# A 31-tap causal convolution split between TensorE and VectorE: 16 and 15 taps in place of 19 and 12

## What is computed

```
proj = h @ w_in[l]
a_val, a_gate, u_pool, gate_a, gate_b = jnp.split(proj, ...)
ya = a_val * jax.nn.sigmoid(a_gate)              # 256 x 512
ya = causal_dwconv(ya, w_dw_a[l], b_dw_a[l])     # 31 taps, each channel by itself
ya = jax.nn.silu(layer_norm(ya, ln_a_g[l], ln_a_b[l]))
ya = ya @ w_pw_a[l]
pooled = causal_multiscale_pool(u_pool)
yb = jnp.einsum("bsgc,gcd->bsgd", pooled, w_pool[l]).reshape(...) * pool_scale[l]
merged = jax.nn.sigmoid(gate_a) * ya + jax.nn.sigmoid(gate_b) * yb
mix = merged @ w_out[l]
```

## Time and profile before

| | us |
|---|---|
| median of 3 runs | 1150.93 |
| the runs | 1148.71, 1150.93, 1152.8 |
| the profiled execution, its time | 1148.73 |
| its span, from the first to the last instruction | 1146.9 |
| PE busy / DVE busy / ACT busy in the span | 1090.2 / 792.9 / 601.2 |

### The profile page before, as it was taken

One profiled execution on the slowest core, in us unless ns is written; L12 is line 12 of the kernel. 1 busy time (PEld: TensorE's weight loads), 2 busy tenths in 40 slices (PEclk: granted clock), 3 DMA queues, 4 the chain that ended last, 5 costly groups with the idle time before them and its releaser, 6 DMA issues.

```text
span 1146.9 us, 19072 instructions
## 1 busy us (share of the span) xinstructions
PE 1090.2 (95%) x7816; PEld 1021.5 (89%) x7816; DVE 792.9 (69%) x1363; ACT 601.2 (52%) x1016; POOL 3.3 (0%) x13
## 2 busy tenths in 40 slices
PE   7998989999999999879989999999999899999997
PEld 7998878899999989779988799999899787999996
DVE  7988488878877788686675755555688747455555
ACT  5567435465565547643354644454565546444453
POOL 0000000000000000000000000000000000000000
PEclk9999999999999998989999999999999999999999
DMA  9985246346666624233222456555555335555520
GB/s 371 418 330 176 92 148 257 107 153 244 245 210 218 199 79 140 69 104 131 74 92 88 149 172 190 193 184 198 170 184 166 111 110 186 191 189 182 190 73 37
DMA packets 58550, 195.56 MB, mean 171 GB/s; under 512 B 10848, under 2 KB 11232, under 8 KB 58208
## 3 DMA queue, kind: packets, MB, share of 16 engines
q1 hardware_dynamic: 58464, 194.35, 49.6%
HBM read 193.01 MB, written 1.31 MB: 169 GB/s over the span
## 4 chain that ended last, share of the span: by engine, by line
PE 74%; DVE 17%; ACT 6%; issue 2%; SPq 1%; DMA 0%; POOL 0%; ACTq 0%; DVEq 0%; POOLq 0%
PE ps L542 61%; DVE lo L1644 5%; PE ps L816 4%; ACT hi L1119 2%; DVE raw L1631 2%; PE ps L644 2%; PE ps L699 1%; DVE ev L1875 1%; PE ps L537 1%; DVE ev L1872 1%; PE ps L549 1%; DVE B L1653 1%; PE ps L822 1%; DVE B L2039 1%; DVE B L1759 1%
## 5 line engine op out<-in xcount | busy, mean ns | idle before, releaser
L1644 DVE TENSOR_TENSOR lo<-raw,hi 128x1024 fp32r<-128x1024 f32 x311 | 377.1, 1221 | 171.5 <-ACT hi L1119 170.5
L542 PE MATMUL ps<-hh,hi 128*128 128x256 f32 x1568 | 447.8, 286 | 14.6 <-DVE hl L1736 3.2
L542 PE MATMUL ps<-hh,lo 128*128 128x256 f32 x1568 | 441.3, 281 | 0.0
L542 PE MATMUL ps<-hl,hi 128*128 128x256 f32 x1568 | 441.1, 281 | 0.0
L1119 ACT ACTIVATE hi<-raw 128x1024 fp32r<-128x1024 f32 x311 | 322.9, 1051 | 55.2 <-PE ps L542 55.1
L542 PEld LDWEIGHTS ps<-hh,hi 128*128 128x128 f32 x1568 | 298.4, 190 | 20.0 <-issue 10.0
L542 PEld LDWEIGHTS ps<-hl,hi 128*128 128x128 f32 x1568 | 298.3, 190 | 1.9
L542 PEld LDWEIGHTS ps<-hh,lo 128*128 128x128 f32 x1568 | 298.3, 190 | 0.0
L1350 ACT ACTIVATE ev<-ps 128x256 f32<-128x256 f32 x72 | 27.7, 385 | 109.9 <-PE ps L542 109.9
L542 PE MATMUL ps<-hi,fh 128*128 128x512 f32 x192 | 76.3, 398 | 0.0
L542 PE MATMUL ps<-lo,fh 128*128 128x512 f32 x192 | 75.9, 395 | 0.0
(11 more groups left out here) (274 smaller groups left out, 1332.6 us busy)
## 6 DMA issues: line engine op xcount, KB each, us to landing
raw<-in_w SPq DMA_DIRECT2D x359, 512.0 KB, 4.3
B<-in_t SPq DMA_DIRECT2D x2, 512.0 KB, 4.9
xa<-in_x SPq DMA_DIRECT2D x1, 1024.0 KB, 10.5
B<-in_r SPq DMA_DIRECT2D x1, 1024.0 KB, 7.1
out<-h SPq DMA_DIRECT2D x4, 256.0 KB, 2.0
cst<-in_c SPq DMA_DIRECT2D x1, 928.0 KB, 8.5
B<-between SPq DMA_DIRECT2D x32, 4.0 KB, 1.7
vec<-in_v SPq DMA_DIRECT2D x1, 328.5 KB, 6.6
```

The costliest lines, as they stand in the source:

```text
L542: m = g.matmul(o, l, r, start=first and n == 0, stop=last and n == 2, skip_group_check=True)
L1644: g.tensor_tensor(lo[:, j % SPLIT, :], raw[:, PLACE[j] % RAW, :], hi[:, j % SPLIT, :].bitcast(F), ALU.subtract).then_inc(*up("lo", j))
```

## The change

Taps 12, 13 and 14 move from TensorE to VectorE. TensorE's groups 9, 10 and 11 have one tap in place of two. VectorE does two taps in each of its turns 4, 5 and 6 in place of one: taps 9 and 10, 11 and 12, 13 and 14. The joining addition waits for VectorE's tap 14 in place of 11.

```diff
-        PE_TAPS = list(range(12, 31))
-        TAPS_AT = {n: t for n, t in zip(range(1, 13), (1, 1, 1, 2, 2, 1, 2, 2, 2, 2, 2, 1))}
+        PE_TAPS = list(range(15, 31))
+        TAPS_AT = {n: t for n, t in zip(range(1, 13), (1, 1, 1, 2, 2, 1, 2, 2, 1, 1, 1, 1))}
...
                 if n < 7:
-                    tap(4 + n if n < 2 else 5 + n)
+                    for i in (4 + n,) if n < 2 else (5 + n,) if n < 4 else (2 * n + 1, 2 * n + 2):
+                        tap(i)
...
                 s.wait_ge(*at("conv", (30, 3)))
-                s.wait_ge(*at("tap", (11, 3)))
+                s.wait_ge(*at("tap", (14, 3)))
```

## The result

The changed kernel takes 1149.0 us (median of 20 runs) and the kernel before 1151.3 us (20 runs). The ratio is 0.9974 with a 95% interval of 0.9962 to 0.9986: 3.0 us less (1.6 to 4.4), where 5.2 were forecast. Weighted by their half widths (1.4, 1.8 and 1.6 us) the three make 3.4 us, give or take 0.9, so 5.2 lies outside; each of the two later comparisons alone would just admit it (up to 5.3 and 5.5). The change is faster, but a good third of its gain is missing.

A forecast was written before the change was run, and what follows sets the result against it. TensorE was taken to bound the long convolution's stretch; three taps at 1.73 us take 5.19 us off the path, VectorE's added work hidden in waits. 1150.3 less 5.19 gives 1145.1 us, range 1141.5 to 1149.

The forecast's parts named there:

- TensorE's term: In the long convolution, three taps leave TensorE in groups 9, 10 and 11: 3 x 1.73 = 5.19 us off the path.
- VectorE's turns: Two taps in turns 4, 5 and 6, 4.74 us added, fit into VectorE's waits; it ends 0.88 us before TensorE.
- The other end: VectorE's operations at 477 ns each, a pair of taps 3.82 us, VectorE 0.26 us behind TensorE: gain 4.93 us.
- The step that failed: Behind the convolution only the start moves; the next projection's first matmul stays 14.14 us after the addition, span 5.19 us shorter.
- the rival for "slower": Clock halved from the next projection's first matmul for its 96 passes: 11.5 us more, 1156.6 us; chance 0.03.
- The other rival about the clock: After the convolution, one more low-clock stretch eats up to 3.4 us of the gain: around 1148.5 us; chance 0.11.
- The level: Base for the whole kernel: mean of four executions, 1150.3 us, from which 5.19 was taken to give 1145.1.

The follow-up runs named there:

- the two later comparisons: The changed kernel, run unchanged twice more against the kernel before: ratios 0.997 and 0.9966, so 3.5 and 3.9 us less.
- the ladder: One, two, three or four taps moved from TensorE to VectorE, against the kernel before: ratios 0.9994, 0.9972, 0.9974 (first comparison) and 0.9933.
- the shift: 15 matmuls on the idle tile ahead of TensorE's last tap, in the kernel before (1154.18 us) and in the changed kernel (1147.42 us).
- the filling: 60 in place of 38 matmuls on the idle tile ahead of the next projection: kernel before 1152.33 us, changed kernel 1145.67, four taps moved 1143.69.

## Why the prediction was wrong

- **TensorE's term** was right. Three times 1.73 us left the path, in the three groups named, and the joining addition came 5.19 us earlier when the 0.2 us between the executions are taken off.
- **VectorE's turns** were right turn by turn: waits of 1.53 us in turn 5 (1.5 forecast) and none in turn 6, a pair of taps at 3.17 us (3.16), slack 0.89 (0.88). The other end weighed there, each operation at its full recorded 477 ns, would have made a pair 3.82; two taps in direct succession don't cost that. The prediction took that end for the rule of the Trainium skill (VectorE: DVE Perf Modes, "The DRAIN you can't avoid"), but gave only half of it: the section says that the next operation waits for an empty pipe, and also that one that is not held starts earlier. The trace of the changed kernel, with 0.396 us from start to start, agrees with the second part.
- **The step that failed** is the one behind the convolution: "TensorE idles there now too and loses nothing". The idle time is indeed the same 2.8 us, but whether it costs clock depends on when it comes, and the change moved it to where it does. It cost 1.54 us in each of three traces. The kernel before lost nothing at this place in two traces, but did lose it (10.20 us for the 72 matmuls) once 15 matmuls had moved the place by 1.75 us; the changed kernel with the same 15 matmuls took 8.66 again.
- **The rivals.** The fall of the clock at exactly this place stood there as the rival for "slower", with 3 in 100. The place was right; the price of 11.5 us supposed that the low clock would last through the projection, where it lasted 3.4 us. The other rival about the clock, a part of the gain eaten, with 11 in 100, is nearest to what happened. It named no place, priced a stretch at up to 3.4 us where this one cost 1.54, and took the stretches for chance. I argued against it that as many stretches can vanish as appear. For a single idle stretch that is moved by a fixed amount, that was wrong. What I leaned on was the Trainium skill (TensorE: Matmul & The Clock Gate, "Part 1"), which says that the gate doesn't start anew with the kernel and that the number of slow matmuls varies from run to run. The traces here agree that executions of one kernel differ (a mean clock of 0.983, 0.983 and 0.981 in the three of the changed one). That the losses therefore even out at a given place was my own step, and the traces disagree with it: the outcome here was the same in three traces of one kernel and in two of the other.
- **The sum with this term:** 5.19 - 1.54 = 3.65 us, or 3.5 with the 0.17 us around the span, against 3.4 measured over three comparisons. Within the first comparison, 3.0 (1.6 to 4.4), it fits too.
- **The level.** The forecast of 1145.1 started from a mean of four executions, 1150.3. Over 20 runs the kernel before has 1151.3, so another 1.0 us of the miss is the base. The profiled execution of 1148.73 us is very likely the first of the three runs, 1148.71, counted twice; the mean of the three is 1150.8.

What stays open: each trace is one execution, so that the half-clock stretch falls here in the timed runs as well is inferred from the times of the ladder and the shift, not seen in each. Moving the idle time moves everything behind it as well, and the filling, which was to test this one gap alone, came with another half-clock stretch ahead of it; so the share of this gap in the timed gain rests on the traces and on the sum coming out. The half-clock stretches further behind also differ between traces (the first pair ended only 1.1 us apart in span, the second pair 2.8). From the last of the projection's 72 matmuls to the end of the span the kernel before takes 985.8 and 988.3 us, the changed kernel 988.6, 988.5 and 989.0, and the other variants between 987.0 and 990.8. What the change does to that part, if anything, no run tells. Why a gap is caught at one place and not at another isn't shown either.

## What to carry to other kernels

Shortening work on the path moves every idle stretch of TensorE behind it, and such a stretch (here 2.8 us, ahead of dense matmuls) can start or stop costing clock by being moved. So look at the granted clock right behind each such gap before and after, price a caught one from a row (here 1.54 us for 3.4 us at half clock), and judge an edit by several sizes of it: one, two, three and four taps gave -0.7, -3.2, -3.4 and -7.7 us. VectorE's work that stayed inside its measured waits was free, and carrying the order of time forward by hand foretold what was left of them to some hundredths of a microsecond.

## What was not expected of the hardware

The half-clock stretch at the projection recurs in place relative to the work in all three traces of the changed kernel, within some 0.3 us of the first matmul, although one execution lay 2.4 us earlier in its span than the others. And useless matmuls can be free: 15 of them (1.75 us) ahead of the last tap left the changed kernel no slower (0.9957 against 0.9966). In the trace they give back 1.54 us, since the idle time no longer lies where it was caught.
